# Prompt head norm placed beside the samples' matrix memory, row-form sums there, value pages split one page earlier, and the output projection started by column halves

## What is computed

```python
# 8 attention heads (differential, paged K/V cache of 4096 keys per sample), 4 mLSTM heads (256 wide)
# mLSTM, one chunk, state C0 (256x256) and n0 (256) per sample and head:
s   = einsum(q, k) * exp(d - m)
num = w_inter * (q @ C0) + s @ v
den = w_inter * (q @ n0) + sum(s)
h   = num / maximum(abs(den), exp(-m))
C   = w_c * C0 + einsum(w_s, k, v)          # n likewise
# end of the mixer
a     = rms_norm(a_heads, attn_out_norm) * (1 - lam_init)       # per head of 128
m_out = rms_norm(h, mlstm_out_norm) * sigmoid(og)               # per head of 256
x     = x + concat(a, m_out) @ w_out
x     = x + square(relu(rms_norm(x, norm_ffn) @ w_up)) @ w_down
```

## Time and profile before

| | us |
|---|---|
| median of 3 runs | 3967.59 (3961.88 to 3968.80) |
| the profiled execution | 3977.39 |
| its span | 3975.5 |
| mean granted TensorE clock in it | 0.949 of full |
| sample_mlstm | 1043.5 to 1174.9 |
| decode_attention | 1174.9 to 2126.5 |
| finish_and_project, up to its first output tile | 2126.5 to 2192.5 |

### The profile page before, as it was taken

One profiled execution on the slowest core, in us unless ns is written; L12 is line 12 of the kernel. 1 busy time (PEld: TensorE's weight loads), 2 busy tenths in 40 slices (PEclk: granted clock), 3 DMA queues, 4 the chain that ended last, 5 costly groups with the idle time before them and its releaser, 6 DMA issues. The chain is left out here.

```text
span 3975.5 us, 65864 instructions
## 1 busy us (share of the span) xinstructions
PE 3661.7 (92%) x26386; PEld 3380.6 (85%) x26386; DVE 1781.6 (45%) x2761; ACT 1285.9 (32%) x1879; POOL 717.6 (18%) x436
## 2 busy tenths in 40 slices
PE   8999998867778999999986999999999999999998
PEld 7999996545677777777762999999999999999998
DVE  4222224754446666666665334333333333333333
ACT  3111111432006777777762213222222222222221
POOL 0000000000005777777782000000000000000000
PEclk9999999668769999999996999999999999999999
DMA  7443332035527888888873432223222223222221
GB/s 208 110 110 108 107 86 102 27 92 157 146 95 277 297 306 299 302 298 298 303 264 107 132 82 85 85 86 91 91 85 85 85 88 94 85 85 85 85 86 66
DMA packets 454555, 564.87 MB, mean 142 GB/s; under 512 B 39846, under 2 KB 330580, under 8 KB 453772
## 3 DMA queue, kind: packets, MB, share of 16 engines
q1 hardware_dynamic: 454316, 561.53, 44.8%
HBM read 515.00 MB, written 46.47 MB: 141 GB/s over the span
## 5 line engine op out<-in xcount | busy, mean ns | idle before, releaser
L1561 POOL TENSOR_TENSOR dc_vl<-dc_vpages,dc_vh 128x1024 fp32r<-128x1024 f32 x256 | 609.4, 2383 | 90.0 <-ACT dc_vh L1894 83.3
L71 PE MATMUL f_acc<-xf_hi,ffn_hi 128*128 128x272 f32 x2048 | 594.2, 290 | 0.0
L69 PE MATMUL f_acc<-hidden_hi,ffn_lo 128*128 128x272 f32 x2048 | 591.6, 289 | 2.8 <-DVE mix_t L2319 2.8
L71 PE MATMUL f_acc<-hidden_hi,ffn_hi 128*128 128x272 f32 x2048 | 592.9, 289 | 0.0
L69 PE MATMUL f_acc<-xf_hi,ffn_lo 128*128 128x272 f32 x2048 | 591.4, 289 | 0.5
L70 PE MATMUL f_acc<-hidden_lo,ffn_hi 128*128 128x272 f32 x2048 | 590.7, 288 | 0.0
L70 PE MATMUL f_acc<-xf_lo,ffn_hi 128*128 128x272 f32 x2048 | 588.5, 287 | 0.0
L71 PE MATMUL z_acc<-xn_hi,win_hi 128*128 128x280 f32 x1536 | 448.1, 292 | 0.0
L69 PE MATMUL z_acc<-xn_hi,win_lo 128*128 128x280 f32 x1536 | 446.9, 291 | 1.1 <-DVE win_lo L302 1.1
L70 PE MATMUL z_acc<-xn_lo,win_hi 128*128 128x280 f32 x1536 | 446.8, 291 | 0.0
L2270 ACT ACTIVATE ffn_hi<-ffn_raw 128x2048 fp32r<-128x2048 f32 x127 | 242.4, 1908 | 619.4 <-PE f_acc L71 619.4
(11 more groups left out here) (362 smaller groups left out, 6336.2 us busy)
## 6 DMA issues: line engine op xcount, KB each, us to landing
dc_kpages<-in_cache_k SPq DMA_DIRECT2D x256, 512.0 KB, 5.0
dc_vpages<-in_cache_v SPq DMA_DIRECT2D x256, 512.0 KB, 4.7
ffn_raw<-in_w_up SPq DMA_DIRECT2D x64, 1024.0 KB, 6.3
ffn_raw<-in_w_down SPq DMA_DIRECT2D x64, 1024.0 KB, 5.0
win_raw<-in_w_in SPq DMA_DIRECT2D x48, 1024.0 KB, 6.3
ffn_raw<-in_w_out SPq DMA_DIRECT2D x16, 1024.0 KB, 6.3
z_scratch<-z_out SPq DMA_DIRECT2D x48, 280.0 KB, 2.4
sm_c<-in_state_C SPq DMA_DIRECT2D x32, 256.0 KB, 4.7
```

Of the source, the lines that this page charges most:

```text
L69: nc.tensor.matmul(out, wlo, xhi, start=first, stop=False)
L71: return nc.tensor.matmul(out, whi, xhi, start=False, stop=last)
L1561: G.tensor_tensor(vl[:, m % VBUF, :], vring[:, m % RING, :], vh[:, m % VBUF, :].bitcast(F32), ALU.subtract).then_inc(vlo, 1)
```

## The change

In **sample_mlstm** the numerators become rows: the queries are laid into a padded tile `sm_qpad` (32 columns a sample, zero but for that sample's own 4 queries), and 16 matmuls with `sm_qpad` as weights and the state's 257 columns as moving operand accumulate into one PSUM tile of 32 rows; column 257 is the denominator. One matmul adds `sw x v`. DVE divides the 32 rows, PE turns them back (`sm_turned`), DVE puts them into `mix`. The small loads and the states have semaphores of their own, and the states no longer wait for `sm_v`. The weights of head h+1 are made in the middle of head h's updates.

The **head norm and gating of the prompt's 512 columns** are added to that stage: 16 squares on ACT (128x512), 16 gathering matmuls (12x512) after the updates of heads 0, 1 and 2 (6, 6 and 4), four `og` loads of 512 KB, four sigmoids of 128x1024, one root of 12x512, a reciprocal and four gating products on DVE, a store of the 12 inverse rows to a scratch tensor and 12 loads that broadcast one row each over 128 partitions (`ph_spread`), ahead of head 3's state stores in the SP queue, and 16 scalings of 128x512 on DVE at the stage's end.

In **decode_attention** `VBUF` is 4, and each value page is loaded and split one page earlier.

In **finish_and_project** only the 32 sample columns are normed and gated, in a few wide instructions. The high and low parts are made by halves of 272 columns; the first half of tiles 0 to 7 before the norm, and PE's first output tile waits for each half by itself. The first weight tile goes ahead of `og` (now 128 bytes a run) and the gains, and the residual comes in four quarters.

```diff
 def load(sp, h):
...
+        def load_states(sp, h):
             for b in range(NB):
-                get(c0[s][:, b, :, 0:MD], a["state_C"][0, b, h].rearrange("(e p) n -> p e n", p=P))
+                sp.dma_start(c0[h][:, b, :, 0:MD], a["state_C"][0, b, h].rearrange("(e p) n -> p e n", p=P))\
+                    .then_inc(c_in[h], 16)
...
-            sp.wait_ge(ones_made, 2 * d.hm)
             for h in range(d.hm):
-                load(sp, h, h)
+                load(sp, h)
+                load_states(sp, h)
+                if h == 1:
+                    for i in range(d.hm):
+                        sp.dma_start(og[i][:, :, :], ogv[cog // E + i][:, :, N_META:TP]).then_inc(og_in[i], 16)
...
             for h in range(d.hm):
+                if h == d.hm - 1:
+                    sp.wait_ge(inv_made, 1)
+                    sp.dma_start(inv_dram, inv[:, :]).then_inc(inv_out, 16)
+                    sp.wait_ge(inv_out, 16)
+                    for i in range(NH):
+                        sp.dma_start(spread[:, i, :], inv_dram[i:i + 1, :].to_broadcast([P, S])).then_inc(spread_in, 16)
...
+            weigh(0)
             for h in range(d.hm):
+                divide(h)
                 for b in range(NB):
...
+                    if b == 1:
+                        put(h)
+                    if b == 3 and h + 1 < d.hm:
+                        weigh(h + 1)
+                if h == d.hm - 2:
+                    invert()
+                    for i in range(d.hm):
+                        gate(i)
...
+            for n in range(d.kc):
+                norm(n)
...
+                for b in range(NB):
+                    for k in range(E):
+                        nc.tensor.matmul(num[0:TS, 0:MD + 1], qpad[s][:, k, b * TS:(b + 1) * TS],
+                                         c0[h][:, b, k, :], start=(b == 0 and k == 0), stop=False)
...
-    RING, VBUF = 4, 3
+    RING, VBUF = 4, 4
...
+        split_page = lambda s, i: 2 * (pair_of(s) + 1) + 1 + i
...
-                    if LAG - 1 <= s < SLOTS - 1:
-                        v_low(2 * (pair_of(s) + 1) + i)
+                    if 0 <= split_page(s, i) < NP:
+                        v_low(split_page(s, i))
...
+            for n in range(N // 2):
+                split(0, n)
+            act.wait_ge(og_in, 16)
+            nc.scalar.activation(og[:, :, :], og[:, :, :], ACT.Sigmoid).then_inc(sigmoid_made, 1)
             act.wait_ge(rooting, 1)
             nc.scalar.activation(root[:, :], root[:, :], ACT.Sqrt).then_inc(rooted, 1)
...
                     if first and j == 0 and h == 0:
                         pe.wait_ge(lo_made, k + 1)
+                    elif first and j == 0:
+                        pe.wait_ge(lo_made, N + k + 1)
```

More of the change, by code:

```diff
@@ L1311, in _ @@
                                     pattern=[[-NS, NB], [0, NS]], channel_multiplier=1).then_inc(own_made, 1)
+            nc.gpsimd.memset(gather[:, :, :], 0.0).then_inc(gather_made, 1)
+            pool.wait_ge(gather_made, 1)
+            for i, width in enumerate((d.vd, MD)):
+                nc.gpsimd.memset(gather[:, i, NH - 1:NH], 1.0 / width).then_inc(gather_made, 1)
         @block.vector
@@ L1425, in _ @@
                             pe.wait_ge(state_new, i - 3)
-                        nc.tensor.matmul(acc[i % 4][:, 0:MD + 1], kw[s][:, b, e * P:(e + 1) * P], v[h][:, :],
+                        elif i == 0:
+                            pe.wait_ge(states_put, 1)
+                        nc.tensor.matmul(acc[i % 4][:, 0:MD + 1], kw[h % 2][:, b, e * P:(e + 1) * P], v[h][:, :],
                                          start=True, stop=True).then_inc(updated, 1)
+                    if b == 1:
+                        turn_out(h)
+                    if b == 2 and h + 1 < d.hm:
+                        scores(h + 1)
+                for n in part(h):
+                    pe.wait_ge(squared, n + 1)
+                    pe.wait_ge(gather_made, 3)
+                    x = head(n)
+                    nc.tensor.matmul(mean[0:NH, 0:S], gather[:, int(n >= d.ha), NH - 1 - x:2 * NH - 1 - x], sq[n % 6][:, :],
+                                     start=(n == 0), stop=(n == d.kc - 1)).then_inc(gathered, 1)
             pe.wait_ge(new_put, d.hm)
@@ L2149, in _ @@
-            V.reciprocal(inv[0:NH, :], root[:, :]).then_inc(inverted, 1)
-            def trail(n):
-                dve.wait_ge(hi_made, n + 1)
-                V.tensor_tensor(mlo[:, n, :], mix[:, n, :], mhi[:, n, :].bitcast(F32), ALU.subtract)\
-                    .then_inc(lo_made, 1)
-            for n in range(d.kc):
-                h = head(n)
-                gain = gains[:, 0:1] if n < d.ha else gains[:, 1 + (n - d.ha) % E:2 + (n - d.ha) % E]
-                dve.wait_ge(spread_ready, h + 1)
-                V.scalar_tensor_tensor(two(mix[:, n, :]), two(mix[:, n, :]), gain, spread[h % 2][:, :, 0:d.ohalf],
-                                       ALU.mult, ALU.mult).then_inc(scaled, 1)
-                if n >= 1:
-                    trail(n - 1)
@@ L2164, in _ @@
-            trail(d.kc - 1)
+            V.reciprocal(inv[:, :], root[:, :]).then_inc(inverted, 1)
+            trailing(dve, 0, 0)
+            dve.wait_ge(gated, 2)
+            dve.wait_ge(spread_ready, 1)
+            rows = lambda lo, hi: spread[:, lo * TS:hi * TS].rearrange("p (h t) -> p h t", t=TS)
+            V.scalar_tensor_tensor(smp[:, 0:d.ha, :], smp[:, 0:d.ha, :], gains[:, 0:1], rows(0, d.ha),
+                                   ALU.mult, ALU.mult).then_inc(scaled, 1)
+            heads_m = smp[:, d.ha:N, :].rearrange("p (h e) t -> p e h t", e=E)
@@ L2165, in _ @@
+            for e in range(E):
+                V.scalar_tensor_tensor(heads_m[:, e], heads_m[:, e], gains[:, 1 + e:2 + e], rows(d.ha, NH),
+                                       ALU.mult, ALU.mult).then_inc(scaled, 1)
+            for n in range(N // 2, N):
+                trail(0, n)
+            for n in range(N):
+                trail(1, n)
+                if n == N // 2:
+                    trailing(dve, 1, 1)
             dve_group(dve, 0, True)
```

370 lines of the change are left out of this document (212 added, 158 removed).

## The result

The changed kernel took 3896.48 us (median of 4 runs, 3892.43 to 3897.61) against 3965.99 (4 runs, 3961.88 to 3968.80) for the kernel before: a ratio of 0.9824 [0.9807, 0.9841], 69.5 us less. Forecast were 3883.6 in a range of 3862 to 3915, 84 us less.

The account below looks back on a forecast made before the run. PE was taken as full in most stretches, with thin matmuls in sample_mlstm, waits in decode and a norm chain before the first output tile. -6 - 28 - 50 = -84 takes the median 3967.6 to 3883.6 us, range 3862 to 3915.

Parts of the forecast that it names:

- The update matmul has the same width, so at 2.4 GHz each is 0.44 us: In sample_mlstm: sums' 257-column matmuls priced from the update matmul, 17 x 0.44 = 7.4 us a head; updates also at 0.44.
- If the clock falls in each of the three weight-making gaps: In sample_mlstm: 2.5 us lost at each gap would leave the stage's gain at -3 instead of -10 us.
- The base: Sum made on the 3977.4 us profiled execution, then 9.8 us taken off to reach the median: 3883.6 us.
- -6: Sample_mlstm's forecast term: stage 6 us shorter, taken between -10 and -3.
- Decode, -28: Decode_attention 28 us shorter as PE's wait for POOL's low part goes: 23 steady part, 5 tail; bounds -15 to -38.
- this shutting out of DVE by POOL: In decode: DVE's eight 64x4 subtractions, blocked by POOL, would go from 18.2 to 18.9 us, under 1 us more.
- the prediction's mark for right: In decode's steady part: POOL low-part waits gone, and waits at the turn not grown by more than a third of them.
- Finish, -50: In finish_and_project: PE's first output tile starts near 2142 instead of 2192.6, 50 us earlier; bounds -52 to -46.
- (a): Rival: clock stays at 1.2 GHz in sample_mlstm, stage ends some 42 us later than before, total 3931 us; chance 10%.
- (b): Rival: decode's wait for POOL is only renamed, decode gives 2 to 6 us in its tail, total 3907 us; chance 14%.
- (c): Rival: POOL becomes decode's clock, decode +87 instead of -28 us, total 3999 us; chance 3%.
- (d): Rival: sample_mlstm's broadcast loads land one after another, 101 us instead of 11, total 3967 us; chance 3%.

Follow-up runs that it names:

- pad128: Changed kernel with `sm_kw` and `sm_v` back at 128 partitions, the other 96 zero: 3881.44 us, ratio 0.9777; sample_mlstm 120.6 us.
- after: The changed kernel itself, all parts in, as profiled: 3896.48 us, ratio 0.9824; sample_mlstm 134.8 us, decode 920.5 us.
- again: The kernel before, unchanged, profiled a second time: 3963.28 us; sample_mlstm 123.8 us, decode 948.3 us.
- pages_only: The kernel before with only the decode part: four value buffers, pages loaded and split one page earlier. 3937.51 us, ratio 0.9925.
- before: The kernel without the change, in its first profile: sample_mlstm 131.3 us, decode 951.7 us; median 3965.99 us over 4 runs.
- no_pages: The changed kernel with the decode part undone (`VBUF` 3 again): 3928.34 us, ratio 0.9900; decode 955.1 us.
- late_half: The changed kernel, but the first output tile waits for both halves of all low parts: 3909.33 us, ratio 0.9845.
- Best: Changed kernel padded to 128 rows, prompt's norm rearranged into idle gaps of sample_mlstm, finish's root ahead of gating: 3873.97 us, ratio 0.9765.
- rows_only_pad: The kernel before with the row-form sums alone, without the prompt's norm, updates padded to 128 partitions: 3935.26 us, ratio 0.9922.

## Why the prediction came out as it did

**The step that failed** is "The update matmul has the same width, so at 2.4 GHz each is 0.44 us". The width is the same; the rows are not, and the working never looked at them, though the code cuts both tiles from `P` to `TS` partitions. The two order excerpts hide it, since they print the output's shape alone (`sm_acc` 128x257 on both sides). The clause "If the clock falls in each of the three weight-making gaps" put the right symptom on the lesser cause: the clock falls inside the updates with PE busy, and the gap costs it only where the rows have not, as in head 2 of pad128. It was priced at 3 x 2.5 us; the heads measured 27.6 us against 23.45 and 23.31 with the rows restored. With the rows restored the rest of the sum stands: forecast were 23.1 us a head, 21.3 with four gathers, and a last DVE row at 1160.5, and pad128 has 23.45, 23.31 (the head whose gap cost the clock) and

```profile
1149.17 10.69 DVE L1416 SCALAR_TENSOR_TENSOR mix_t<-mix_t,ph_gains,ph_spread 128x512 f32<-128x512 f32 x16
1159.78 0.47 DVE L1456 COPY sm_nrows<-sm_acc 32x128 f32<-32x128 f32 x2
```

against 1171.17 in after. That is the bulk of the miss.

**The base.** The sum was made against a profiled execution, and its 9.8 us above the median were taken off at the end, as if they lay outside the changed stages. `again` shows that most of the surplus lay inside, and other runs bear it out: pages_only, whose sample_mlstm is that of before, has 123.9 us there, and no_pages and late_half, with that of after, 133.4 and 134.9. Against `again` sample_mlstm could win only 2.8 us even with every step of the forecast right: its last DVE row stands at 1162.91, 119.7 us behind the stage's start, and the forecast's 1160.5 is 116.9 behind. Of the 17 us between -6 and +11, 14.2 are thus the rows (134.8 against 120.6) and 3 the base.

**Decode, -28.** Right in sum (-27.8 against `again`, -31.2 against the first profile), wrong in its two terms, whose errors cancel by luck. Forecast were 23 from the steady part and 5 from the tail. From POOL's first half of the scores (L1570, L1687) to the start of its seven pages in a row at the end the traces give 874.5 us in `again` and 846.2 in after: -28.3. The tail from there to the finish is 46.9 and 47.2: nothing. POOL's tail, first of `again`, then of after, with the last of DVE's 64x4 subtractions of the earlier trace rows in each, and PE's longest wait in after's tail:

```profile
2085.67 4.69 POOL L1561 TENSOR_TENSOR dc_vl<-dc_vpages,dc_vh 128x1024 fp32r<-128x1024 f32 x2 [0.85 <-ACT dc_vh L1894]
2092.34 11.65 POOL L1561 TENSOR_TENSOR dc_vl<-dc_vpages,dc_vh 128x1024 fp32r<-128x1024 f32 x5 [1.97 <-ACT dc_vh L1894]
2071.37 1.84 DVE L1800 TENSOR_TENSOR dc_eff<-dc_beyond,dc_low 64x4 f32<-64x4 f32 x1
```

```profile
2068.30 4.69 POOL L1678 TENSOR_TENSOR dc_vl<-dc_vpages,dc_vh 128x1024 fp32r<-128x1024 f32 x2 [2.18 <-ACT dc_vh L2011]
2074.96 9.36 POOL L1678 TENSOR_TENSOR dc_vl<-dc_vpages,dc_vh 128x1024 fp32r<-128x1024 f32 x4 [1.97 <-ACT dc_vh L2011]
2051.58 14.55 DVE L1917 TENSOR_TENSOR dc_eff<-dc_beyond,dc_low 64x4 f32<-64x4 f32 x1
2069.15 0.76 PE L1759 MATMUL dc_pout<-dc_vh,dc_php 128*128 128x512 f32 x1 [6.03 <-DVE dc_own_rows L1901]
```

One page fewer is there (9.36 against 11.65, the forecast 2.3), but the same seven-page run is still ahead of it, and in that run the gain was lost again. DVE's subtraction lasts 14.55 us in after, up to the end of POOL's seven pages (2049.81 to 2066.12), where it lasted 1.84 in `again`. ACT and DVE make the last probabilities behind it, so PE stops for 6.03 us (2.39 in `again`), and POOL's wait for ACT is 1.3 us longer instead of gone. The prediction had named this shutting out of DVE by POOL and priced it at under 1 us; the eight subtractions took 31.1 us instead of 18.2, in after and in pages_only. PE's last eight matmuls also run at a lower clock (0.50, in `again` 0.66). In the steady part more was given back than the prediction's mark for right allowed, a third of 39.4: the waits at the turn rose by 17.7 us, and those for DVE's low part of a key page by 6.6 (from 3.1). Yet the gain was larger than 23, and the reason seems to be that a wait costs more than its bracket. In 770 against 800 us PE's idle time fell by only 13.8 us (70.0 to 56.2), its busy time by 16.2. The row of before ahead of the wait of the earlier trace rows:

```profile
1474.69 0.39 PE L1642 MATMUL dc_pout<-dc_vh,dc_php 128*128 128x512 f32 x1
```

The next matmul starts at 1475.56, 0.87 us later, where these matmuls otherwise follow each other at 0.23 (1475.84, 1476.08 and 1476.31 behind it). The wait cost 0.64 us, and its bracket says 0.47: 0.17 is counted as busy time, since the record of 0.39 us ahead of the wait is not overlapped by the next one. Taken over all 88 waits in the trace of before, the starts lie 0.155 us further apart than their usual 0.234 and the bracket together, 13.6 us in all. The 770 us of after have none of these waits, so 13.6 of the 16.2 us are accounted for; no run tested it by itself.

**Finish, -50.** Right in its steps: og ready at 6.7 us into the stage (7.5 forecast), the root at 8.4 (9.5), leading's end at 10.4 (11.5), the spreads' end at 14.4 (15.5), the tile at 14.3 (15 to 16). No stall follows: 195.3 us from first tile to last addition in `again` and in after. The Trainium skill (ScalarE: Activation LUTs, "Table sets: the hidden batching unit") holds that each switch between sets costs a load, and the trace agrees in part. Of the finish's two loads of 1.28 us the first is over before og lands and costs nothing; the second, at 2104.17, lies on the path to the root, which starts at 2105.46, so the switch takes 1.30 us here and not the 2.66 that the prediction quotes. Best takes the root ahead of the gating, and its first tile starts 2.5 us earlier in the stage. (The working says that its sum holds no table load; it holds 1.28 us ahead of either root.)

**The rivals.** (a), the clock stays at 1.2 GHz in sample_mlstm: in part. Its mechanism is there for updates and gathers but not for the sums, which are 7.12 us at 1.00, and it cost 14 of the 48 us that lie between this rival and the forecast. (By the working's own terms, 7.2 us more in four sums, 6.7 in three heads' updates and 13.3 in the gathers, less the 2.5 us lost at first and the forecast's own 10, the rival's stage ends some 50 us later, not 42.) For it the prediction named "gaps and 32-column weights"; the sums have 32-column weights and hold the clock, so in this kernel those weights are not it. (b), the decode wait only renamed: some 24 us of it were, but pages_only and no_pages show 28 to 35 us gained in the stage. (c), POOL becomes decode's clock: refuted; POOL's waits for ACT halved. (d), broadcasts one after another at 8.4 us: refuted. In pad128 DVE's reciprocal ended at 1134.51, and the gains' scaling stands at

```profile
1148.98 0.15 DVE L1413 TENSOR_SCALAR ph_gains<-ph_gains 128x1 f32<-128x1 f32 x1 [2.44 <-DMA ph_spread<-inv_scratch]
```

so the store and all 12 loads took 14.5 us; 13 were forecast (2 + 11). In after, where the updates are slower, they were in time without any wait (the gains' scaling at 1160.38, right behind the updates).

## What to carry to other kernels

When a change shrinks an operand, write the new shape of every matmul beside the old one, rows and columns, before reusing its duration; the same columns are not the same matmul, and zero rows that look like waste may be what keeps PE fast. Cost a stall on PE by the distance from start to start, not by its bracket alone, and ask of a tail which engine's run of pages remains, and which engine cannot work beside it. A profiled execution that is longer than the median has its surplus somewhere: look for it in a second trace before taking it off evenly.

## What the runs showed of the hardware

With PE busy throughout, fp32 matmuls of 257 columns ran at a granted clock of 1.00 with 128 rows (2.87 us for 12 records) and fell to 0.50 with 32 (5.50), in the same place of the same kernel; the added rows were zero. With 64 rows they held 1.00 in that place (2.86) and fell in head 3 (8.99 us for 24 records, 5.44 with 128 rows), with PE busy in 7.10 of 7.10 us at 0.50. The thin matmuls of before, 128 rows but 4 columns, stood at 0.50 too.

The Trainium skill (TensorE: Matmul & The Clock Gate, "What's actually happening") says that the gate sets the clock by how busy PE has recently been. With busy as the profile counts it, the trace does not agree: the stretch at 1096 to 1101 of after is busy in 5.00 of 5.00 us and stands at 0.50. The gaps of rows_only_pad (2.46 us, with 128 rows; then 3.65, 3.31 and 2.80 us for 8 records) agree with the page, but pad128 kept the clock behind two gaps of that length (1.97 us) and lost it behind the third (3.54); what decides between them is open.

In decode_attention a DVE subtraction of 64x4 took as long as POOL's page instructions beside it went on: in after seven of the eight took 2.35 to 2.37 us and ended within 0.02 us of one page's end, and the eighth took 14.55 us, up to the end of a run of seven pages.
